# Norm weights through GpSimd's queue, their transposition ahead of x, first weights rounded panel by panel, first step's products by their inputs

## The reference

```
h      = rmsnorm(x) * g1                        # x: 512 + 64 rows of 1024
qa, ka, va, qb, kb, vb, gates = split(h @ w_in) # w_in: 1024 x 4352
oa     = sliding window attention(qa, ka, va)   # 8 heads, window 128, T5 bias, sinks
ob     = stick breaking attention(qb, kb, vb)   # 8 heads, causal
merged = sigmoid(gates[:1024]) * (oa @ w_proj_a) + sigmoid(gates[1024:]) * (ob @ w_proj_b)
x      = x + merged @ w_out
u      = square(relu(rmsnorm(x) * g2 @ w_up))   # w_up: 1024 x 4096
x      = x + u @ w_down
y      = rmsnorm(x) * g_final                   # and the new rows of the key/value caches
```

## Time and profile before

| | us |
|---|---|
| median of 3 runs | 836.43 (836.32 to 836.47) |
| the profiled execution | 836.16 |
| its span | 834.3 |
| around the span | 1.9 |
| TensorE busy | 822.9 of the span |
| mean granted TensorE clock | 0.996 |

### The profile page before, as it was taken

One profiled execution on the slowest core, in us unless ns is written; L12 is line 12 of the kernel. 1 busy time (PEld: TensorE's weight loads), 2 busy tenths in 40 slices (PEclk: granted clock), 3 DMA queues, 4 the chain that ended last, 5 costly groups with the idle time before them and its releaser, 6 DMA issues.

```text
span 834.3 us, 16017 instructions
## 1 busy us (share of the span) xinstructions
PE 822.9 (99%) x6205; PEld 807.0 (97%) x6205; DVE 624.6 (75%) x1075; ACT 391.4 (47%) x668; POOL 294.6 (35%) x213
## 2 busy tenths in 40 slices
PE   9999999999999999999999999999999999999996
PEld 7999999999999989999999999999999999999995
DVE  5597876356889999876337988488966889479996
ACT  5657775244667757644342433243433343333532
POOL 2562222225545444354434300642025400552330
PEclk9999999999999999999999999999999999999998
DMA  8742112441112111143313113422134113422203
GB/s 278 253 160 89 52 51 65 152 165 51 51 54 93 57 50 51 50 164 127 100 53 101 52 51 102 152 87 66 50 101 137 64 50 101 132 69 67 83 2 114
DMA packets 68449, 78.18 MB, mean 94 GB/s; under 512 B 2552, under 2 KB 65072, under 8 KB 68016
## 3 DMA queue, kind: packets, MB, share of 16 engines
q1 hardware_dynamic: 68080, 76.92, 28.1%
q10 hardware_dynamic: 320, 0.60, 0.2%
HBM read 70.15 MB, written 8.93 MB: 95 GB/s over the span
## 4 chain that ended last, share of the span: by engine, by line
PE 88%; DVE 9%; issue 2%; ACT 1%; DVEq 0%; ACTq 0%
PE pan L1565 56%; PE pan L1781 12%; PE att L1781 10%; PE att L1719 1%; PE att L1692 1%; PE pan L1621 1%; DVE sp_lo L1159 1%; PE att L1709 1%; PE att L1565 1%; DVE sp_hi L1157 1%; DVE xT L1398 1%; PE pan L1601 1%; PE att L1861 1%; PE pan L1654 1%; DVE ob_lo L1221 1%
## 5 line engine op out<-in xcount | busy, mean ns | idle before, releaser
L474 POOL TENSOR_TENSOR w_lo<-raw,w_hi 128x512 fp32r<-128x512 f32 x160 | 222.0, 1412 | 425.4 <-ACT w_hi L816 182.4
L1565 PE MATMUL pan<-a_lo,w_hi 128*128 128x288 f32 x624 | 133.8, 295 | 0.0
L1565 PE MATMUL pan<-a_hi,w_hi 128*128 128x288 f32 x624 | 133.8, 296 | 0.0
L1565 PE MATMUL pan<-a_hi,w_lo 128*128 128x288 f32 x624 | 133.1, 294 | 0.0
L1565 PE MATMUL pan<-h_hi,w_hi 128*128 128x288 f32 x512 | 110.5, 298 | 0.0
L1565 PE MATMUL pan<-h_lo,w_hi 128*128 128x288 f32 x512 | 109.5, 295 | 0.0
L1565 PE MATMUL pan<-h_hi,w_lo 128*128 128x288 f32 x512 | 108.5, 293 | 0.0
L1565 PEld LDWEIGHTS pan<-a_hi,w_hi 128*128 128x128 f32 x624 | 99.9, 188 | 1.0
L1565 PEld LDWEIGHTS pan<-a_hi,w_lo 128*128 128x128 f32 x624 | 100.8, 188 | 0.0
L1565 PEld LDWEIGHTS pan<-a_lo,w_hi 128*128 128x128 f32 x624 | 99.6, 188 | 0.0
L1781 PE MATMUL pan<-F_hi,w_hi 128*128 128x288 f32 x320 | 96.4, 301 | 0.6 <-DVE xT L1398 0.6
(11 more groups left out here) (283 smaller groups left out, 1768.9 us busy)
## 6 DMA issues: line engine op xcount, KB each, us to landing
raw<-in_w_in SPq DMA_DIRECT2D x34, 512.0 KB, 4.6
raw<-in_w_up SPq DMA_DIRECT2D x32, 512.0 KB, 4.8
raw<-in_w_down SPq DMA_DIRECT2D x32, 512.0 KB, 4.7
raw<-in_w_out SPq DMA_DIRECT2D x8, 512.0 KB, 3.9
x_spill<-xT SPq DMA_DIRECT2D x1, 2304.0 KB, 7.1
xT<-x_spill SPq DMA_DIRECT2D x1, 2304.0 KB, 10.9
x_rows<-in_x_prompt SPq DMA_DIRECT2D x4, 512.0 KB, 6.8
raw<-in_w_pa SPq DMA_DIRECT2D x4, 512.0 KB, 3.9
```

What stands on the lines that cost most here:

```text
L474: last = nc.gpsimd.tensor_tensor(w_lo[:, slot, k:k + 4, :], raw[:, rs, k:k + 4, j * P:(j + 1) * P], w_hi[:, slot, k:k + 4, :].bitcast(F32) ...
L1565: got = nc.tensor.matmul(out[:, h, 0:HALF], w, x[:, h * HALF:(h + 1) * HALF], start=first and n == 0, stop=last and n == 2)
```

## The change

The two loads of g1 and g2 are issued by GpSimd, as its first instructions, and no longer by ScalarE. TensorE transposes them before tile 0 of x. ScalarE rounds the first half of the first weights in two instructions of 512 elements, panel 0 (semaphore w_panel_0) and then panel 1. VectorE makes a_lo of tile 0 before a_lo of the samples. TensorE makes the 8 products of tile 0 one by one, each when its own inputs are there, and ahead of the transposition of tile 2.

```diff
--- before.py
+++ after.py
@@ -183,6 +183,7 @@
         x_in, xs_in = [sem("x_in%d" % q) for q in range(4)], sem("xs_in")
         w_first = [sem("w_first0"), sem("w_first1")]
         xa_ready = sem("xa_ready")
+        w_panel_0 = sem("w_panel_0")
         warm_ready, xs_out, xs_scaled, xs_hi, hs_ready, xs_ready = (sem("warm_ready"), sem("xs_out"), sem("xs_scaled"), sem("xs_hi"),
                                                                     sem("hs_ready"), sem("xs_ready"))
         ident_in, grow_in, const_in = sem("ident_in"), sem("grow_in"), sem("const_in")
@@ -468,6 +469,9 @@
 
         @block.gpsimd
         def _(pool):
+            pool.dma_start(grow[0:KT, :], g1.rearrange("(k p) -> k p", p=P)).then_inc(grow_in, 16)
+            pool.dma_start(grow[KT:2 * KT, :], g2.rearrange("(k p) -> k p", p=P)).then_inc(grow_in, 16)
+
             def split(slot, rs, j, ready):
                 pool.wait_ge(w_hi_ready, ready)
                 for k in range(0, KT, 4):
@@ -562,8 +566,6 @@
                 round_w(first_panel(b) + 4 + j, j, b + 2 + (j // 2))
 
             act.dma_start(ident[:], consts[:, 0:P]).then_inc(ident_in, 16)
-            act.dma_start(grow[0:KT, :], g1.rearrange("(k p) -> k p", p=P)).then_inc(grow_in, 16)
-            act.dma_start(grow[KT:2 * KT, :], g2.rearrange("(k p) -> k p", p=P)).then_inc(grow_in, 16)
             act.preload_act_table(ACT.Sqrt)
             act.wait_ge(zero_ready, 1)
             act.wait_ge(gcol_ready, 1)
@@ -594,7 +596,9 @@
                 if k == 0:
                     act.wait_ge(xs_scaled, 1)
                     nc.scalar.activation(a_hi[:, :, SEQ:TOK], xs_g[:], ACT.Copy).then_inc(xs_hi, 1)
-                    round_first(0)
+                    act.wait_ge(w_first[0], 16)
+                    nc.scalar.activation(w_hi[:, 0, 0:4, :], raw[:, 0, 0:4, 0:P], ACT.Copy).then_inc(w_panel_0, 1)
+                    nc.scalar.activation(w_hi[:, 1, 0:4, :], raw[:, 0, 0:4, P:2 * P], ACT.Copy).then_inc(w_hi_ready, 1)
                 elif k == 4:
                     nc.scalar.activation(xT[:, :, SEQ:TOK], att[:, 3, :].rearrange("p (k n) -> p k n", k=KT), ACT.Copy).then_inc(xs_ready, 1)
                 elif k == 2:
@@ -935,14 +939,15 @@
             dve.wait_ge(xs_out, 1)
             nc.vector.tensor_tensor(xs_g[:], att[:, 3, :].rearrange("p (k n) -> p k n", k=KT), gcol[:, 0:KT].unsqueeze(2).to_broadcast([P, KT, NEW]),
                                     ALU.mult).then_inc(xs_scaled, 1)
-            dve.wait_ge(xs_hi, 1)
-            nc.vector.tensor_tensor(a_lo[:, :, SEQ:TOK], xs_g[:], a_hi[:, :, SEQ:TOK].bitcast(F32), ALU.subtract).then_inc(hs_ready, 1)
             for k in range(KT):
                 if k in ACT_X:
                     dve.wait_ge(xa_ready, ACT_X.index(k) + 1)
                 dve.wait_ge(h_hi_ready, k + 1)
                 nc.vector.scalar_tensor_tensor(out=a_lo[:, k, 0:SEQ], in0=x_bank(k), scalar=gcol[:, k:k + 1],
                                                in1=a_hi[:, k, 0:SEQ].bitcast(F32), op0=ALU.mult, op1=ALU.subtract).then_inc(h_ready, 1)
+                if k == 0:
+                    dve.wait_ge(xs_hi, 1)
+                    nc.vector.tensor_tensor(a_lo[:, :, SEQ:TOK], xs_g[:], a_hi[:, :, SEQ:TOK].bitcast(F32), ALU.subtract).then_inc(hs_ready, 1)
                 if k in DVE_X and k < KT - 3:
                     take_x(k)
             for k in range(KT - 3, KT):
@@ -1621,24 +1626,43 @@
                             nc.tensor.matmul(pan[:, j, h, 0:HALF], w_hi[:, j, k, :], x[:, k, h * HALF:(h + 1) * HALF], start=k == 0 and x is a_hi, stop=False)
 
             pe.wait_ge(ident_in, 16)
+            pe.wait_ge(grow_in, 2 * 16)
+            nc.tensor.transpose(pan[:, 1, 1, 0:2 * KT], grow[:], ident[0:2 * KT, 0:2 * KT]).then_inc(gcol_out, 1)
             pe.wait_ge(x_in[0], 16)
             x_out_tile(0)
-            pe.wait_ge(grow_in, 2 * 16)
-            nc.tensor.transpose(pan[:, 1, 1, 0:2 * KT], grow[:], ident[0:2 * KT, 0:2 * KT]).then_inc(gcol_out, 1)
             pe.wait_ge(xs_in, 16)
             for k in range(KT):
                 got = nc.tensor.transpose(att[:, 3, k * NEW:(k + 1) * NEW], x_rows[0:NEW, TT, k * P:(k + 1) * P], ident[0:NEW, 0:NEW])
             got.then_inc(xs_out, 1)
             x_out_tile(1)
             on_zeros(12)
+            pe.wait_ge(gcol_ready, 1)
+
+            def first_product(j, x, h):
+
+                nc.tensor.matmul(pan[:, j, h, 0:HALF], w_hi[:, j, 0, :], x[:, 0, h * HALF:(h + 1) * HALF], start=x is a_hi, stop=False)
+
+            pe.wait_ge(w_panel_0, 1)
+            pe.wait_ge(h_hi_ready, 1)
+            first_product(0, a_hi, 0)
+            pe.wait_ge(xs_hi, 1)
+            first_product(0, a_hi, 1)
+            pe.wait_ge(h_ready, 1)
+            first_product(0, a_lo, 0)
+            pe.wait_ge(w_hi_ready, 1)
+            first_product(1, a_hi, 0)
+            first_product(1, a_hi, 1)
+            first_product(1, a_lo, 0)
+            pe.wait_ge(hs_ready, 1)
+            first_product(0, a_lo, 1)
+            first_product(1, a_lo, 1)
             pe.wait_ge(x_in[1], 16)
             x_out_tile(2)
-            pe.wait_ge(gcol_ready, 1)
-            pe.wait_ge(hs_ready, 1)
             for k in range(KT):
-                if k % 4 == 0:
-                    pe.wait_ge(w_hi_ready, k // 4 + 1)
-                first_step(k)
+                if k == 4:
+                    pe.wait_ge(w_hi_ready, 2)
+                if k:
+                    first_step(k)
                 if k in (1, 3):
                     pe.wait_ge(x_in[(k + 3) // 2], 16)
                 if k + 3 < KT:
```

## The result

| | before | after |
|---|---|---|
| median of 20 runs, us | 836.42 (835.95 to 837.88) | 838.78 |
| ratio to before | | 1.0023 (1.0017 to 1.003) |
| profiled execution | 836.16 | 837.29 |
| its span | 834.3 | 835.5 |

Forecast were 836.2 and a range up to 837.9; the kernel is 2.36 us slower by the medians, and the profiled execution 1.13 us. The ratio is that of the means, 838.47 against 836.53 us, without one execution of 2829 us that never came again.

What follows compares the result with a forecast made beforehand. TensorE, busy 822.9 of 834.3 us, was taken as the bound, so only waits at the start could be regained. Profiled 836.16 us minus 0.25 gave 835.91, plus 0.27 to the median 836.2; range 835.7 to 837.9.

Steps and rivals of the forecast that it cites:

- so I take it as landed before 5.82 us: Norm-weight loads by GpSimd: landed at 5.7 us, in time for TensorE's weight load at 5.86, removing a 0.21 us wait.
- The rival of a first call's 6 us on GpSimd: GpSimd's first load: if fresh code's 6 us held for a DMA, landing past 10 us; no chance of its own.
- Each us later than 5.82 is a us at the end: TensorE behind the zeros: each us of landing past 5.82 us delays everything behind it and the end by one us.
- the break-even point: Landing of the norm weights at 6.07 us, where the predicted gain of 0.25 us is gone.
- the gain is eaten: Rival at the start: landing between 6.07 and 7.7 us, or ScalarE or tile 2 taking all; 0 to +1.6 us, chance 0.31.
- The clock: TensorE idle behind the zeros: a falling clock would add to the slow load's cost; zero products 0.21 us early, 0.12 later.
- the rival of a landing past 7.7 us: Load of grow bounds the start, TensorE idle behind the zeros; up to 4.3 us, 840.7 at the upper bound; chance 0.10.
- slower: Outcome beyond 0.2% (1.67 us), tied to the norm weights landing at 7.7 us or later; chance 0.10.
- The rest of the change: Start, roundings and product order included: step of tile 1 at 11.62 instead of 11.88 us, a gain of 0.26 us.
- What is late next: ScalarE's second rounding at about 11.77, 0.05 us later; step of tile 3 at 14.65 instead of 14.88, leaving 0.23 us.
- The two roundings: ScalarE's w_hi in two instructions of 0.57 us each, 1.14 instead of 0.95 us, costing 0.19 us more.
- The large number: Tile 0's first product on TensorE at 9.28 instead of 10.38 us, 1.1 us earlier, most of it given back by tile 1.

Runs made afterwards that it cites:

- e1: Changed kernel with ScalarE issuing the two norm-weight loads behind ident, instead of GpSimd: 837.12 us, ratio 1.0009.
- e3: Changed kernel with ScalarE issuing the norm-weight loads, grow ahead of ident: 836.94 us, ratio 1.0009.
- e4: Changed kernel with 36 products of zeros at the start instead of 24: 837.58 us, ratio 1.0013.
- e14: e7 with one VectorE memset fewer (qscale set with three instead of four): 836.43 us, ratio 0.9999.
- e8: e5 with the first half of the weights rounded in one instruction of 1024 elements instead of two: 838.01 us, ratio 1.0018.
- e5: e1 with g1 transposed alone, g2 in its own buffer and transposed behind tile 1: 837.83 us, ratio 1.0016.
- e11: Kernel before with the whole change except the loads and the place of grow's transposition: 836.57 us, ratio 1.0002.
- e13: e5 with one VectorE memset fewer (qscale set with three instead of four): 836.82 us, ratio 1.0003.
- e2: Kernel before with only the two norm-weight loads moved to GpSimd: 836.89 us, ratio 1.0008.
- e6: Changed kernel with 16 products of zeros at the start instead of 24: 839.65 us, ratio 1.004.
- e10: Kernel before with SyncE loading ident ahead of x and ScalarE the norm weights first: 836.94 us, ratio 1.0005.
- e12: Kernel before with one purposeless memset more at VectorE's start: 837.37 us, ratio 1.0013.
- e7: e5 with tile 2's transposition back ahead of the first products: 837.71 us, ratio 1.0016.

## Why the prediction was wrong

**The failed step: "so I take it as landed before 5.82 us".** The forecast was 0.76 + 0.29 + 4.62 = 5.7 us; the load landed at 6.96. All three terms were off. GpSimd's first issue starts at 1.28 (+0.52), takes 0.67 (+0.38), and issue to landing is 5.01 (+0.39). The second could have been read from the kernel before, whose own first issue of grow takes 0.66 us:

```profile
1.23 0.66 ACTq L565 DMA_DIRECT2D grow<-in_g  x1
```

The second takes 0.29; I priced a first issue by a second one. Together they cancel what the free queue was to give: the second load goes out at the same time as before, 1.95 against 1.92.

The rival of a first call's 6 us on GpSimd did not come either: its first issue took 0.68 us.

**The rule behind it was right.** "Each us later than 5.82 is a us at the end": S came 1.20 us later, the matmuls at 17.8 us 1.14, and so in e1 (0.83 and 0.77), e3 (1.51 and 1.44) and e4 (1.42 and 1.36); at the end it was 1.11, 0.86, 1.30 and 1.11. What I had weighed too lightly is that the new place takes away 0.7 us of cover: a load that landed at 6.54, while tile 0 was transposed, is now wanted at 5.86. With ScalarE's own loads, whose landing I knew, e1 already costs +0.77. A landing at 6.96 is 6.96 - 6.07 = 0.9 us beyond the break-even point that the prediction named, in the case that it called "the gain is eaten", at 836.8. The profiled 837.29 (837.6 with its 0.27) is that case.

**The clock was named, and not priced.** This is the second failed step: the text had it only in the rival of a landing past 7.7 us, and no term of the sum or of the range's upper end, 837.9, holds it. Ten of the change's 19 executions had a lower mean clock and took 1.4 to 3.3 us more than the profiled one; that is the rest of the 2.36 us, and what carried the median over the range. The late landing alone ends inside it, at 837.29. GpSimd's second load landed between 6.74 and 7.17 us in the four profiles that have it, so the condition that the prediction gave to "slower", a landing from 7.7 on, was probably not needed; the slower executions' own landings are not on record, and why their clock fell stays open.

**The rest of the change did what was forecast, in a smaller size.** From S to the step of tile 1: 6.02 before, 12.92 - 7.06 = 5.86 after, 5.76 forecast. A gain of 0.16 instead of 0.26, since a_lo of tile 1 came 0.62 us behind the start of xT and the step 0.80 behind a_lo's start, each some 0.04 above the forecast. From S to the step of tile 3 the gain was 0.05 and not 0.23. "What is late next" named the right place, ScalarE's second rounding, but put it 5.91 us behind S (11.77 - 5.86); it stands at 13.08 - 7.06 = 6.02, since a_hi of tile 2 waits 0.41 us for the moved transposition, and a_lo of tile 3 and its step follow. e14 says the same from the other side: with that transposition in its old place R is 8.87, a gain of 0.15. The two roundings cost less than forecast, 0.52 us from one to the next against 0.57, and without them R is 0.31 longer (e8).

**The large number was no gain.** The first product went out 1.1 us earlier once the weights were there (e5: 9.31 against 10.38), as forecast, and 0.85 of it was given back by tile 1, as forecast. e11 and e13 bound the whole rest between 0.9993 and 1.0012 of before, and e14, with tile 2 in its old place, between 0.999 and 1.0008.

## What to carry to other kernels

Before an instruction is moved ahead of others on the busiest engine, look up when its input lands, not how long its wait was: the row showed a wait of 0.21 us only because 0.7 us of other work stood in front. Price the first DMA of a queue by a first one (here start 1.28, issue 0.67, landing 5.0 us later for 4 KB by GpSimd), and a wait behind TensorE's first work at more than its length, since in some executions a lower clock may come on top. Do not take one profile for the median: compare its time and mean clock with those of all executions first. A version that should be equal and is 0.1% off may have lost it far from the edit: compare the traces instruction by instruction, and find the place where the difference steps.

## What the runs showed of the hardware

- GpSimd's first DMA issue starts at 1.28 us, 0.52 after ScalarE's and SyncE's first; issue to landing of 4 KB, behind a first load of 4 KB, is 4.8 to 5.2 us (5.00 in e2), against 4.66 by ScalarE at the same moment (e1).
- 64 KB of ident landed 3.5 us after issue when it was the first load of ScalarE's queue, and 5.6 us after (1.73 to 7.33) behind two loads of 4 KB there.
- The same 24 products of zeros end between 5.17 and 6.36 us (e13, e3), as the clock rises at 3.77 or 6.64 us. With 16 of them, and 2.21 us idle behind them, it rose only at 13.41 us (e6).
- After 1.84 us of idle time the clock fell from 2.4 to 1.2 GHz for 3.4 us, in an execution 1.85 us over its kernel's median (e10). The change had a lower mean clock in ten of 19 executions, with 36 zeros in none of 11; what sets this number is not shown.
- A VectorE addition of two numbers a partition took 1.04 us instead of 0.16 where a GpSimd instruction had started 0.27 us ahead of it (e12).
- One VectorE instruction more at the start of the program cost 0.88 us between 93.5 and 94.5 us (the median rose from 836.4 to 837.37); one fewer took 1.0 and 1.3 us from e5 and e7. What delays VectorE there by 0.37 us stays open.
